# A transformer kernel on one Trainium2 core: the gated heads' turn joined into the attention units, the second expert bias in four row groups, the first expert's tokens selected as columns

## The reference, cut to what matters

```python
mod = silu(c) @ w_ada + b_ada                      # six rows of 1024: sh1 sc1 gt1 sh2 sc2 gt2
h = rms_norm(x, g_pre_mix) * (1 + sc1) + sh1
proj = h @ w_in                                    # aq ak av | gq gk gv gg ga
att = sliding_window_sink_attention(aq, ak, av, sinks)
glog = log_sigmoid(ga @ w_gla_gate_up + b_gla_gate) / 16
o = rms_norm(gla_chunked(gq, gk, gv, glog), g_gla_norm) * silu(gg)
x = x + gt1 * rms_norm(concat(att, o) @ w_out, g_post_mix)
h = rms_norm(x, g_pre_ffn) * (1 + sc2) + sh2
top_v, top_i = top_k(h @ w_router + b_router, 4); gates = softmax(top_v)
for each expert e, on the tokens that chose it:
    u = h @ w_mlp1[e] + b_mlp1[e]; a = swiglu(u)
    y += gate * (a @ w_mlp2[e] + b_mlp2[e])
```

## Time and profile before

| | |
|---|---|
| median of three runs | 1760.43 us (1757.78 to 1762.43) |
| the profiled execution | 1759.26 us, its span 1757.3 us |
| PE busy | 1683.3 us (96%) |
| DVE, ACT, POOL busy | 713.4, 499.6, 21.9 us |
| HBM read | 573.5 MB, mean 327 GB/s |
| chain that ended last | PE 65%, DMA 26%, DVE 6%, issue 1%, ACT 1% |

### The profile page before, as it was taken

One profiled execution on the slowest core, in us unless ns is written; L12 is line 12 of the kernel. 1 busy time (PEld: TensorE's weight loads), 2 busy tenths in 40 slices (PEclk: granted clock), 3 DMA queues, 4 the chain that ended last, 5 costly groups with the idle time before them and its releaser, 6 DMA issues.

```text
span 1757.3 us, 21318 instructions
## 1 busy us (share of the span) xinstructions
PE 1683.3 (96%) x8343; PEld 918.0 (52%) x8343; DVE 713.4 (41%) x1019; ACT 499.6 (28%) x712; POOL 21.9 (1%) x49
## 2 busy tenths in 40 slices
PE   6998999999999999999999999997999999999998
PEld 3765633333333333333333333336888797888886
DVE  3555612221212121212121212127666646766665
ACT  3453321211111111111111111115333544553333
POOL 1000000000000000000000000001000000000000
PEclk8998999999999999999999999998999999999999
DMA  9865899999999999999999999997555553446551
GB/s 363 323 232 224 309 386 430 429 428 429 427 430 429 428 429 428 428 429 429 428 429 427 430 429 428 428 416 239 192 185 193 178 204 139 148 149 209 187 179 66
DMA packets 111209, 575.14 MB, mean 327 GB/s; under 512 B 6960, under 2 KB 61296, under 8 KB 81728
## 3 DMA queue, kind: packets, MB, share of 16 engines
q1 hardware_dynamic: 108464, 564.75, 80.3%
q0 software_dynamic: 2368, 8.76, 1.6%
q10 hardware_dynamic: 336, 1.07, 0.2%
HBM read 573.50 MB, written 1.05 MB: 327 GB/s over the span
## 4 chain that ended last, share of the span: by engine, by line
PE 65%; DMA 26%; DVE 6%; issue 1%; ACT 1%; SPq 0%; DVEq 0%; ACTq 0%
DMA ring<-in_w_mlp 23%; PE PS L994 18%; PE PS L654 9%; PE PS L1058 8%; PE PS L981 7%; PE PS L1088 6%; PE PS L1061 4%; PE PS L691 2%; DMA ring<-in_w_ada 2%; DMA ring<-in_ffn_w_up 1%; PE PS L974 1%; PE PS L871 1%; PE PS L942 1%; PE PS L595 1%; PE PS L959 1%
## 5 line engine op out<-in xcount | busy, mean ns | idle before, releaser
L994 PE MATMUL PS<-ring,scr 128*64 128x512 f32 x2176 | 501.1, 614 | 9.4 <-DMA ring<-in_w_mlp 9.4
L994 PEld LDWEIGHTS PS<-ring,scr 128*64 128x64 f32 x2176 | 149.1, 134 | 341.7 <-issue 311.3
L981 PE MATMUL PS<-ring,scr 128*64 128x512 f32 x1088 | 250.1, 602 | 0.0
L1522 ACT ACTIVATE w_hi<-ring 128x2048 fp32r<-128x2048 f32 x90 | 172.4, 1916 | 232.8 <-PE PS L1061 129.3
L2077 DVE TENSOR_TENSOR w_lo<-ring,w_hi 128x2048 fp32r<-128x2048 f32 x90 | 206.0, 2289 | 79.2 <-ACT w_hi L1522 79.1
L2035 DVE TENSOR_SCALAR scr<-iota,scr 128x128 f32<-128x128 f32 (+1 forms) x68 | 20.5, 344 | 404.8 <-PE PS L994 404.3
L2046 DVE TENSOR_SCALAR scr<-PS 64x512 f32<-64x512 f32 x68 | 46.4, 683 | 336.8 <-PE PS L994 335.6
L1469 ACT ACTIVATE scr<-scr 64x512 f32<-64x512 f32 x68 | 42.4, 623 | 485.2 <-DVE scr L2046 485.2
L1058 PE MATMUL PS<-HT_both,w_hi 128*128 128x512 f32 x640 | 159.9, 392 | 0.0
L981 PEld LDWEIGHTS PS<-ring,scr 128*64 128x64 f32 x1088 | 72.4, 137 | 149.3 <-issue 149.3
L1058 PEld LDWEIGHTS PS<-HT_both,w_hi 128*128 128x128 f32 x640 | 116.2, 189 | 21.6
(11 more groups left out here) (342 smaller groups left out, 1737.4 us busy)
## 6 DMA issues: line engine op xcount, KB each, us to landing
ring<-in_w_mlp SPq DMA_DIRECT2D x204, 2048.0 KB, 21.6
ring<-in_w_ada SPq DMA_DIRECT2D x24, 1024.0 KB, 9.4
ring<-in_ffn_w_gate SPq DMA_DIRECT2D x22, 1024.0 KB, 5.3
ring<-in_ffn_w_up SPq DMA_DIRECT2D x22, 1024.0 KB, 5.4
ring<-in_ffn_w_down SPq DMA_DIRECT2D x22, 1024.0 KB, 4.8
ring<-in_w_in SPq DMA_DIRECT2D x19, 1024.0 KB, 5.3
ring<-in_w_out SPq DMA_DIRECT2D x8, 1024.0 KB, 5.4
ring<-in_w_gate SPq DMA_DIRECT2D x8, 1024.0 KB, 5.0
```

The costliest lines, as they stand in the source:

```text
L981: mm = pe.matmul(PS[c * CAP:(c + 1) * CAP, 6, :], aT[:, h, k, :], w[:, k, c * HALF:(c + 1) * HALF], start=(h == 0 and k == 0), stop=(h == ...
L994: mm = pe.matmul(PS[c * CAP:(c + 1) * CAP, 4 + h, :], xsT[:, 2 * (j % 2) + k, j // 2, :], w[:, k, h, c, :], start=False, stop=(j == 3 and ...
L1522: act.activation(w_hi[:, at % PAIRS, :], raw(n), ACT.Copy).then_inc(hi_ready, 1)
```

## The change

1. `LOAD1` has all eight w_ada chunks of the last third ahead of the four w_out chunks.
2. The attention's values are made by `cols_out` (24 matmuls of 256 columns), copied, turned by two transposes and copied again.
3. The gated heads are turned in two pieces inside the attention: pair 0 in unit 3 and pair 1 in unit 5, both into bank 0, with ACT's copy and DVE's low part in units 4 and 5. ACT splits the first w_out chunk behind the move of unit 4 and no longer ahead of it.
4. `ada_sum` takes four matmuls at a time (two sums and not four), into four banks, later than before.
5. POOL's waits: the first small loads wait for the use of chunk "ga" (before: w_ada chunk 4); router and expert biases wait for the attention's values and for the second sum.
6. Gates are turned by four matmuls into four groups of 32 rows; `b_mlp2` is laid out likewise, and `second_bias` is four matmuls in four row groups, followed by four `keep_busy` matmuls.
7. The first expert's tokens are selected straight as columns: 16 matmuls with 128 x 128 pieces of H (every second column) as stationary tile and `sel` as moving one; gather, one ACT copy and the turn fall away.

```diff
-            ADA(2, range(4)) + OUT[:1] + ADA(2, range(4, 6)) + OUT[1:2] + ADA(2, range(6, KC)) + OUT[2:]
+            ADA(2) + OUT
...
-            pool.wait_ge(weights_used, used1(in1("ada", 0, 4)))
+            pool.wait_ge(weights_used, used1(in1("ga")))
...
-            pool.wait_ge(gla_pe, 6)
+            pool.wait_ge(s_o[0], NU)
             pool.dma_start(wr, kp(a["w_router"][0])).then_inc(load_wr, 16)
+            for g in range(4):
+                pool.dma_start(b1[g * E:(g + 1) * E, :], a["b_mlp1"][0]).then_inc(load_moe, 16)
             pool.wait_ge(ada_ps, N_ADA_PS)
...
-            def ada_sum(m):
+            def ada_sum(third):
 
-                pe.wait_ge(ada_sb, m // 2 + 1)
-                if m > 2:
-                    pe.wait_ge(ada_ev, 2 * (m - 2))
-                for h in range(2):
-                    g = 32 * (2 * (m % 2) + h)
-                    pe.matmul(PS[:, 6 + h, :], ones[g:g + 1, :], apart[m // 2][g:g + 1, :],
+                pe.wait_ge(ada_sb, third + 1)
+                if third > 1:
+                    pe.wait_ge(ada_ev, 4 * (third - 1))
+                for q in range(4):
+                    pe.matmul(PS[:, 4 + q, :], ones[32 * q:32 * q + 1, :], apart[third][32 * q:32 * q + 1, :],
                               start=True, stop=True).then_inc(ada_ps, 1)
...
-            rows_out(n, pair, P, P, 0, 6, S)
-            rows_out(n, pair, P, P, 1, 6, S + P).then_inc(weights_used, 1)
+            cols_out(n, pair, P, P, 6, S).then_inc(weights_used, 1)
...
+            pe.wait_ge(ev1_dve, 4)
+            for t in range(TT):
+                mm = pe.transpose(PS[:, 6, t * P:(t + 1) * P], vT[:, t * P:(t + 1) * P], ident[:])
+            mm.then_inc(rows_ps, 1)
...
                     ada_part(2, range(2 * u - 4, 2 * u - 2), 1)
+                    if u == 3:
+                        pe.wait_ge(gla_dve, G_GATED)
+                        turn_gated(0)
+                    elif u == 5:
+                        pe.wait_ge(mix_lo, 1)
+                        turn_gated(1)
             attention(0, beside)
-            pe.wait_ge(gla_dve, G_GATED)
-            for h in range(GH):
-                for t in range(TT):
-                    mm = pe.transpose(PS[:, 4 + h // 2, (h % 2) * S + t * P:(h % 2) * S + (t + 1) * P],
-                                      og[:, h % 2, t, h // 2, :], ident[:])
-            mm.then_inc(gla_pe, 1)
-            ada_sum(2)
             pe.wait_ge(ada_sb, 3)
             pe.wait_ge(mix_lo, 2)
...
-                for h in range(2):
-                    pe.matmul(PS[:, 2 * t + h, :], GT[:, t * P:(t + 1) * P], b2[:, h * HALF:(h + 1) * HALF],
+                for g in range(4):
+                    pe.matmul(PS[:, g, :], GT[g * E:(g + 1) * E, :], b2[g * E:(g + 1) * E, :],
                               start=True, stop=False, skip_group_check=True)
...
                 if opening:
-                    second_bias(0)
+                    second_bias()
+                    keep_busy(4, 6)
...
-            gather(main)
-            keep_busy(3, 2)
-            pe.wait_ge(main.xs, 1)
-            turn_tokens(main)
-            keep_busy(3, 2)
+            for j in range(2):
+                for k in range(2):
+                    for h in range(2):
+                        at = (2 * (2 * j + k) + h) * CAP
+                        cols = slice(h * HALF + 2 * j * P + k, h * HALF + 2 * (j + 1) * P, 2)
+                        for t in range(TT):
+                            mm = pe.matmul(PS[:, 4, at:at + CAP], H[:, t, cols], sel[:, t, :],
+                                           start=(t == 0), stop=(t == TT - 1))
+            mm.then_inc(main.xsps, 1)
+            pe.sem_inc(main.gather, 1)
+            keep_busy(4, 2)
...
+            def gated_copy(pair):
+
+                act.wait_ge(gla_pe, 6 + pair)
+                act.activation(HT1_hi[:, 4 + 2 * pair:6 + 2 * pair, :], bank2(0), ACT.Copy).then_inc(gla_act, 1)
+
+            def behind(u):
+
+                if u == 4:
                     high1(10)
-                elif u == 5:
                     ada(2)
-                    high1(11)
-            attention(0, HT1_hi, beside)
+                    gated_copy(1)
+            attention(0, HT1_hi, beside, behind)
```

More of the change, by code:

```diff
@@ L840, in _, with turn_gated @@
             pe.wait_ge(consts, N_CONST)
-            pe.wait_ge(ev1_dve, 6)
+            pe.wait_ge(ev1_dve, 7)
+            def turn_gated(pair):
+                for h in (2 * pair, 2 * pair + 1):
+                    for t in range(TT):
+                        mm = pe.transpose(PS[:, 0, (h % 2) * S + t * P:(h % 2) * S + (t + 1) * P],
+                                          og[:, h % 2, t, h // 2, :], ident[:])
+                mm.then_inc(gla_pe, 1)
             def beside(u):
@@ L902, in logits @@
                 mm.then_inc(r_lg, 1)
+            pe.wait_ge(ada_ev, 8)
             keep_busy(3, 4)
@@ L925, in turn_gates, with second_bias @@
                 pe.wait_ge(r_dve, R_G)
[L926 to L927 removed]
+                for g in range(4):
+                    mm = pe.matmul(PS[g * E:(g + 1) * E, 3, 0:P], G[:, g // 2, :], ident[:], start=True, stop=True)
                 mm.then_inc(r_pe, 1)
[L930 removed]
+            def second_bias():
                 pe.wait_ge(r_act, 2)
[L933 to L934 removed]
+                for g in range(4):
+                    pe.matmul(PS[:, g, :], GT[g * E:(g + 1) * E, :], b2[g * E:(g + 1) * E, :],
                               start=True, stop=False, skip_group_check=True)
@@ L1007, in expert_pass @@
                 turn_hidden(0, 6)
-                if opening:
-                    second_bias(1)
-                else:
+                if not opening:
                     scatter((1,))
@@ L1316, in bank2, with attention @@
                 return PS[:, b, :].rearrange("p (k n) -> p k n", k=2)
-            def attention(z, dst, fill):
+            def attention(z, dst, fill, behind=lambda u: None):
                 def exps(u):
@@ L1340, in attention @@
                     evac(u - 1)
+                    behind(u - 1)
                 evac(NU - 1)
@@ L1877, in beside @@
                 elif u >= 4:
-                    low1(6 + u)
+                    if u == 5:
+                        low1(10)
+                    dve.wait_ge(gla_act, A_MIXT - 5 + u)
+                    rows = slice(2 * u - 4, 2 * u - 2)
+                    dve.tensor_tensor(HT1_lo[:, rows, :], bank2(0), HT1_hi[:, rows, :].bitcast(F32),
+                                      ALU.subtract).then_inc(mix_lo, 1)
             attention(0, beside, first=heads)
             attention_low(0, HT1_hi, HT1_lo)
-            for b in range(2):
-                dve.wait_ge(gla_act, A_MIXT - 1 + b)
-                rows = slice(4 + 2 * b, 6 + 2 * b)
-                dve.tensor_tensor(HT1_lo[:, rows, :], bank2(4 + b), HT1_hi[:, rows, :].bitcast(F32),
-                                  ALU.subtract).then_inc(mix_lo, 1)
+            low1(11)
             dve.wait_ge(load_bada2, 4 * 16)
```

44 lines of the change are left out of this document (21 added, 23 removed).

## The result

The changed kernel takes 1745.24 us (median of four runs, 1744.49 to 1747.32), the kernel before 1761.18 in the runs beside it (1757.78 to 1762.43). The ratio is 0.9914 with a 95% interval of 0.9897 to 0.9932: faster, within the forecast's range of 1736 to 1751 and 3.2 us above the forecast of 1742.0. The profiled execution took 1744.81, its span 1742.7.

A forecast was written before the change was run, and what follows sets the result against it. The prediction took the expert weight stream to run at the DMA queue's rate, so time saved before the first pass's end moves the kernel's end one for one; terms summed to -17.3, from 1759.26 to 1742.0, range 1736 to 1751.

The forecast's parts named there:

- Small loads later: Gate matmul at about 52 us: new wait for the late loads, +2.6; queue freed in the first 30 us, -0.5.
- Values as columns: First mixer's attention values: 48 narrow matmuls become 24 wide ones, -2.6, with the transposes hidden under gg1's load.
- End of the attention: First mixer: output tiles start at 139.3 and not 152.08, `mix_done` at 160.0 against 175.05, -15.1.
- the replay: Step-by-step timing of PE, ACT and DVE from 130 us on, putting the first output tile at 139.3.
- Rival 2: End of the attention: hand-overs between PE, ACT and DVE serialise, half of the 15.1 is lost, 1749.6; chance 0.17.
- First selection: From selection to first expert: 5.5 us where it was 4.16, +1.3, bounds +0.4 and +2.6.
- Second bias: First expert pass: second matrix starts at 219.8, not 221.18, -1.3; half clock gone, 5.35 becomes 3.65, -1.7.
- The rule on transfers: Small loads: a fixed cost of about 2.0 us plus bytes by rate, making the gate matmul's wait nothing.
- rival 1: Gate matmul: the small loads land in 2.1 and hold nobody, wait 0, 1739.4; chance 0.13.
- Rival 3: Behind the wait at 52 us the clock falls to 1.2 GHz; slower, 1772 if it lasts to 87; chance 0.03.

The follow-up runs named there:

- experiment 1: Changed kernel with POOL's first wait put back to w_ada chunk 4, so the small loads are where they were; 1741.01 us.
- experiment 9: Kernel before with one edit: POOL waits for the use of chunk "ga" before loading the five small tensors; 1766.37 us.
- Experiment 5: Changed kernel with the first mixer's attention values computed as rows again, without the transposes and the added copy; 1748.77 us.
- experiment 3: Changed kernel with the old order of loads, two w_out chunks between the last w_ada chunks; 1753.62 us.
- experiment 4: Changed kernel with both pairs of gated heads turned behind the attention as before, new order of loads kept; 1750.82 us.
- experiment 6: Changed kernel with the first expert's tokens selected as rows and transposed behind a copy, as before; 1745.79 us.
- experiment 8: Changed kernel with the second bias in its former form and no filling matmuls; 1748.91 us.
- experiment 7: Changed kernel without the filling matmuls behind the second bias in the first pass; 1744.38 us.
- experiment 11: Changed kernel, old selection, no fillers, fourth modulation row ahead of the gains' product, small loads behind the last block of w_ada's first third; 1738.16 us.

## Why the prediction was right, and where it was off

The direction, the size and the mechanism held. The forecast's sum was -17.3; the profiled executions differ by 14.45 (1759.26 to 1744.81), and by 15.0 at the end of the first pass. That time saved ahead of this end moves the end of the kernel one for one holds within the scatter of 2.9 us behind it (1525.5 to 1528.4). Term by term:

- **Small loads later, +2.6 for the wait and -0.5 for the queue ahead.** This is the step that failed. The wait was 3.81, not 2.6, since the load took 5.9 to land and not 4.7: I took the fastest of four rows, in a stretch where the queue is as full, when their median was 5.9. And the clock fall, which I kept in the range at 1.7 and out of the sum, happened: 2.07 for the gate matmul where 1.13 was the price, and in the chain of waits 10.15 for the 48 matmuls behind it where 8.63 was, together 2.5. The queue ahead gave 0.9 (in the chain of waits the w_ada chunk issued at 20.36 takes 9.02, before 9.93). Net +5.3 at the values of the attention, where the sum had +2.1. The sum's 0.5 for the queue, with 1 as its upper bound, was too low as well: PE's w_ada matmuls behind chunk "ga" start at 44.85 to 46.19 in the nine executions with late loads, 45.6 on average, and at 46.89, 47.06 and 47.26 in the three with the loads at 20 us. Experiments 1 and 9 put the net price at the end of the first pass at 4.15 and 4.8.
- **Values as columns, -2.6.** The group is 5.92 against 8.35, -2.4, and the shift from there to the turn of unit 3 gives -2.7. The size held, the reason for it only in part. The transposes were to lie under gg1's transfer, but with PE later that transfer is off the path: they are in the chain of waits with 0.4. A wait of 0.58 for DVE that the kernel before has at 98.57 is gone in return. That the two cancel is luck. Experiment 5 confirms the 2.4.
- **End of the attention, -15.1.** From unit 3 to DVE's start behind the sixth tile the change gains 15.6 (the shift goes from +2.7 to -12.9). The replay had the first output tile at 139.3 in the times of before; with the shift of 2.7 that is 142.0, and it came at 142.06. So close a hit is partly luck: the replay starts ACT's split of the first w_out chunk at once, and the 1.11 that it waited just filled what the replay had left free behind it. Experiments 3 and 4 divide it: 8.6 hang on the order of loads and up to 3.8 on the joined turn, of which 1.6 is a clock fall that may not be its own. The remaining 3.2 or more I put down to two sums in place of four and to their later place; that was not taken out by itself, and is not shown. Rival 2 did not happen in the profiled execution, but experiments 6 and 8 show it to be real in some: the hand-over through ACT's split has about 0.2 us of slack.
- **First selection, +1.3.** It was +0.6: 0.124 per instruction, between the contiguous 0.113 and the strided 0.143 from which I worked; near the lower bound. The rule of the Trainium skill (TensorE: Matmul & The Clock Gate, LDWEIGHTS), by which the column count alone sets the load's timing, gave +0.4: closer than my take. Whether the rest is the stride is not shown, since the row of 0.113 differs in its moving columns too (128 against 64). Experiment 6 shows the same 0.6.
- **Second bias, -1.3 and -1.7 for the clock.** The pass gained 2.7 of the 3.0: the four matmuls in four row groups (eight passes) took 1.14 (1.07 in the chain of waits), the second matrix starts 20.8 after the first expert's beginning and not 21.8, and the clock stays at 1.00. The four fillers were priced at 0.9 and took 1.1; experiment 7 shows that 0.7 of it was given away.
- **The rule on transfers**, from the Trainium skill (DMA: Bandwidth & Descriptors, anatomy of one DMA): by a fixed cost of 2.0 us the wait would have been nothing, which was rival 1. The trace refutes it here: 3.3 to 6.1 for all five loads, in a queue whose DMA share is near 1.
- **Rival 3** (slower through the half clock) had the right mechanism and a small price: the clock came back some 5.4 us after the wait's end, under dense work.

## What to carry to other kernels

Moving a small load from a place where it disturbs to one just ahead of its use buys little and can cost much: here 0.9 to 1.4 us of queue against a net loss of 4 to 5 us by wait and clock. Take for its landing the median of the loads in an equally full stretch, not the fastest, and give it a place with room to spare: experiment 11 issues the gate matrix over 16 us ahead of its use. When PE idles a few microseconds in a dense stretch, count the half clock into the sum. Look at the order of loads first where a stage ends in such a stall: here it was worth 8 us.

## What the runs showed that I had not expected

- The half clock follows an idle stretch of PE of 1.8 us as well as one of 3.8 (experiment 8 and the changed kernel), and one of 1.30 in experiment 4. But 1.32 ahead of L730 in experiment 1 was not followed by one, nor was 1.30 at the place of experiment 4 in the kernel before, nor 1.85 ahead of its L726. The same gap is cheap in one execution and costs a microsecond in another.
- The clock also falls without any idle time: in experiment 8 PE is busy throughout from 206 on, mostly with matmuls of 32 rows; the clock is 0.92 in the window 208 to 210 and 0.50 from 210 to 216. With the same work in four row groups (1.14 us) it stays at 1.00, even with a wait of 0.34 and one of 0.56 behind it (experiment 7).
- Four fp32 matmuls of 512 columns in four separate row groups take 1.14 us together (L948 in PE's timeline), where two in one took 1.98.
- In a full queue the size of a small load says little of when it lands: 1 KB and 64 KB took 5.9 and 5.6 in the first 30 us of the kernel before. In the changed kernel the 1 KB load, the first of the five, took 3.3, but the 4 KB one took 5.8 and the 64 KB one 6.1.
